# A diffusion trunk layer: its first norm taken on token rows, and its first projection run with the k tile outermost

## What is computed

```python
mod = silu(cvec) @ w_ada + b_ada            # 6 vectors of D: sh1, sc1, g1, sh2, sc2, g2
h = x * rsqrt(mean(x * x, axis=-1) + EPS) * rms1_g * (1 + sc1) + sh1
u = h @ w_in                                # q, k, v, the pooling input, the conv input
```

## Time and profile before

| | |
|---|---|
| median of 3 runs | 3322.55 us (3313.8 to 3324.69) |
| profiled execution | 3326.58 us, span 3324.5 us |
| TensorE busy | 2942.1 us, 88% of the span |
| VectorE, ScalarE, GpSimd busy | 1978.3, 1460.9, 459.5 us |
| HBM traffic | 570.72 MB read, 28.31 MB written, 180 GB/s over the span |

### The profile page before, as it was taken

The page is one execution under the profiler, slowest core; times in us unless marked ns, Lnnn a source line. Parts: engine busy times, 40 slices in busy tenths (PEclk is TensorE's granted clock), DMA queues, the critical chain, the costliest instruction groups (busy, mean ns, idle before and its releaser), DMA issues.

```text
span 3324.5 us, 42592 instructions
## 1 busy us (share of the span) xinstructions
PE 2942.1 (88%) x16896; PEld 2267.9 (68%) x16896; DVE 1978.3 (60%) x1880; ACT 1460.9 (44%) x1588; POOL 459.5 (14%) x259
## 2 busy tenths in 40 slices
PE   5979887999985999999859798879999859999997
PEld 4978764887883666666549787648878836666664
DVE  3198874211135888888632988742111358888885
ACT  4135553211124677777442355432111246777774
POOL 0321110000001122122203211100000011222122
PEclk8989998999997999999979999889999979999998
DMA  6211124212125999999832111242222259999994
GB/s 239 69 55 45 45 72 169 77 64 64 64 89 187 335 367 380 370 367 379 305 124 58 53 45 45 96 146 77 64 64 64 89 202 335 375 374 369 373 373 165
DMA packets 238382, 601.12 MB, mean 181 GB/s; under 512 B 13536, under 2 KB 116096, under 8 KB 237472
## 3 DMA queue, kind: packets, MB, share of 16 engines
q1 hardware_dynamic: 224896, 549.09, 45.4%
q0 software_dynamic: 10272, 34.26, 4.0%
q10 hardware_dynamic: 3072, 15.73, 1.2%
HBM read 570.72 MB, written 28.31 MB: 180 GB/s over the span
## 4 chain that ended last, share of the span: by engine, by line
PE 78%; DVE 11%; DMA 5%; ACT 2%; issue 2%; SPq 1%; POOL 0%; DVEq 0%; ACTq 0%; POOLq 0%; PEldq 0%
PE ps L1254 19%; PE ps L1255 19%; PE ps L1256 19%; PE ps L1292 8%; DVE zc L941 4%; DMA raw<-in_w_ada 2%; PE ps L1417 2%; PE ps L1393 1%; DMA xg<-h_dram,next_token 1%; PE ps L1567 1%; PE ps L1406 1%; DMA raw<-in_w_in 1%; PE ps L1337 1%; DVE w_lo L850 1%; DVE stats L971 1%
## 5 line engine op out<-in xcount | busy, mean ns | idle before, releaser
L1254 PE MATMUL ps<-h_hi,w_hi 128*128 128x320 f32 x1408 | 448.3, 318 | 81.1 <-DVE h_lo L899 48.0
L1169 DVE TENSOR_TENSOR m_lo<-m_raw_b,m_hi 128x2048 fp32r<-128x2048 f32 x192 | 439.4, 2289 | 73.4 <-ACT m_hi L794 71.6
L1169 DVE TENSOR_TENSOR m_lo<-m_raw_a,m_hi 128x2048 fp32r<-128x2048 f32 x192 | 438.8, 2288 | 69.7 <-ACT m_hi L794 67.7
L794 ACT CAST m_hi<-m_raw_b 128x2048 fp32r<-128x2048 f32 x192 | 367.1, 1912 | 179.0 <-PE ps L1256 179.0
L1255 PE MATMUL ps<-h_lo,w_hi 128*128 128x320 f32 x1408 | 441.2, 313 | 0.0
L1256 PE MATMUL ps<-h_hi,w_lo 128*128 128x320 f32 x1408 | 440.8, 313 | 0.0
L794 ACT CAST m_hi<-m_raw_a 128x2048 fp32r<-128x2048 f32 x192 | 366.4, 1911 | 164.6 <-PE ps L1256 161.5
L1254 PE MATMUL ps<-m_hi,xs_hi 128*80 128x512 f32 x1024 | 409.1, 400 | 3.3 <-DVE xs_lo L1184 3.3
L1255 PE MATMUL ps<-m_lo,xs_hi 128*80 128x512 f32 x1024 | 406.4, 397 | 0.0
L1256 PE MATMUL ps<-m_hi,xs_lo 128*80 128x512 f32 x1024 | 404.4, 395 | 0.0
L500 ACT CAST w_hi<-raw 128x2048 fp32r<-128x2048 f32 x68 | 129.2, 1902 | 552.4 <-DMA raw<-in_w_gate 335.7
(11 more groups left out here) (257 smaller groups left out, 4744.7 us busy)
## 6 DMA issues: line engine op xcount, KB each, us to landing
m_raw_a<-in_w SPq DMA_DIRECT2D x192, 1024.0 KB, 7.4
m_raw_b<-in_w SPq DMA_DIRECT2D x192, 1024.0 KB, 7.4
raw<-in_w_in SPq DMA_DIRECT2D x72, 512.0 KB, 4.7
raw<-in_w_ada SPq DMA_DIRECT2D x64, 512.0 KB, 4.7
raw<-in_w_gate SPq DMA_DIRECT2D x48, 512.0 KB, 6.2
m_raw_a<-in_w_ada SPq DMA_DIRECT2D x8, 1024.0 KB, 9.6
m_raw_b<-in_w_ada SPq DMA_DIRECT2D x8, 1024.0 KB, 15.6
raw<-in_w_proj_a SPq DMA_DIRECT2D x16, 512.0 KB, 4.1
```

The costliest lines, as they stand in the source:

```text
L794: nc.scalar.copy(m_hi[:, n % RING], m_raw(slot)).then_inc(s["m_high"], 1)
L1169: nc.vector.tensor_tensor(m_lo[:, r], m_raw(slot), m_hi[:, r].bitcast(F32), ALU.subtract).then_inc(s["msplit"], 1)
L1254: pe.matmul(out, wh, xh, start=first, stop=False, skip_group_check=True)
```

## The change

The row scale 1/rms of the first norm is taken from `xtok`, by token rows, where it is one number per partition: ScalarE squares a token tile with a running sum (`accum_out`), VectorE and ScalarE finish the five numbers per tile on [128, 1] columns, and VectorE scales `xtok` in place (`row_scales`), after TensorE has turned the unscaled tile for `x`. TensorE then turns the scaled `xtok` again, k tile by k tile, into two PSUM halves (`turn_h`), ScalarE applies scale and shift while it reads PSUM and writes a new tile `hm`, casts it at once (`high_of`), VectorE subtracts (`low_of`). The first unit (`pool_first`) runs with the k tile outermost and takes each tile as its low part is done; tile k+2 is turned between the matmuls of tile k and tile k+1. The other units run as before; the loop of three passes becomes one written-out pass and a loop of two.

Around it: x is loaded in five DMAs, one per token tile with a semaphore each, by SP in both layers; in layer 1 SP waits for the last scatter itself. The layer's constants `sm` and the first unit's weight chunk go ahead of the eight `w_ada` chunks in SP's queue, and POOL loads neither x nor constants. In layer 1 both weight splits stand ahead of the row statistics; in layer 0 the first stands behind them and the second between h tiles 2 and 3. PSUM banks of the first modulation part move from 6 and 7 to 0 and 1. The second norm of a layer is left as it was.

The diff, cut to its core:

```diff
             sp.dma_start(c_in[:], cvecs).then_inc(s["const_in"], 16)
             sp.dma_start(fold[:], fold_in).then_inc(s["const_in"], 16)
-            sp.dma_start(xtok[:, 0:4, :], x_sample[0].rearrange("(t p) d -> p t d", p=P)).then_inc(s["x_in"], 16)
-            sp.dma_start(xtok[:, 4, :], x_prompt[0]).then_inc(s["x_in"], 16)
+
+            def load_x(lat, ctx):
+
+                for t in range(TT):
+                    src = lat[t * P:(t + 1) * P] if t < 4 else ctx
+                    sp.dma_start(xtok[:, t, :], src).then_inc(s[f"x_in{t}"], 16)
+
+            load_x(x_sample[0], x_prompt[0])
+            sp.dma_start(sm[:], small[0]).then_inc(s["small_in"], 16)
             sp.sem_inc(s["raw_free0"], 1)
             sp.sem_inc(s["raw_free1"], 1)
...
+            def first_wide(l):
+
+                wide(0, in_v[l, POOL0 // CW])
+
+            first_wide(0)
+            for i in range(RAWS):
+                sp.dma_start(m_raw(i), ada_chunk(0, 0, i)).then_inc(s[f"mfull{i}"], 16)
             for l in range(DEPTH):
                 for n, c0 in enumerate((POOL0, CONVB0, CONVA0)):
                     for u in range(2):
-                        wide(u, in_v[l, c0 // CW + u])
+                        if n + u:
+                            wide(u, in_v[l, c0 // CW + u])
+                    if l and n == 0:
+
+                        sp.wait_ge(s["scattered"], 32 * EXPERTS * l)
+                        seen.settle()
+                        load_x(mid_lat, mid_ctx)
...
                 if l + 1 < DEPTH:
+                    sp.wait_ge(s["small_free"], l + 1)
+                    sp.dma_start(sm[:], small[l + 1]).then_inc(s["small_in"], 16)
+                    first_wide(l + 1)
                     for i in range(RAWS):
                         sp.wait_ge(s["msplit"], seen("msplit"))
...
-                pool.wait_ge(s["small_free"], seen("small_free"))
-                seen.settle()
-                pool.dma_start(sm[:], small[l]).then_inc(s["small_in"], 16)
...
-                    pool.dma_start(xtok[:, 0:4, :], mid_lat.rearrange("(t p) d -> p t d", p=P)).then_inc(s["mid_in"], 16)
-                    pool.dma_start(xtok[:, 4, :], mid_ctx).then_inc(s["mid_in"], 16)
...
-                bank = (6, 6, 7)[n]
+                bank = (0, 6, 7)[n]
...
-            def h_high(k):
-
-                act.wait_ge(s["hnorm"], seen("hnorm"))
-                nc.scalar.copy(h_hi[:, k], mm_[:, k]).then_inc(s["row_c"], 1)
+            def x_out(t):
+
+                act.wait_ge(s["tr_in"], TT * l + t + 1)
+                b = 2 * (t % 2)
+                nc.scalar.copy(x[:, :, t * P:(t + 1) * P], flat[:, b * 512:b * 512 + D].rearrange("p (k n) -> p k n", n=P)).then_inc(s["tr_out"], 1)
+
+            def x_stats():
+
+                for t in range(TT):
+                    act.wait_ge(s[f"x_in{t}"], 16 * (l + 1))
+                    nc.scalar.activation(xsq[:, t], xtok[:, t], ACT.Square, accum_out=st[:, 8 + t:9 + t]).then_inc(s["x_sq"], 1)
+                    if t:
+                        x_out(t - 1)
+                    act.wait_ge(s["x_var"], TT * l + t + 1)
+                    nc.scalar.activation(st[:, 13 + t:14 + t], st[:, 8 + t:9 + t], ACT.Sqrt).then_inc(s["x_root"], 1)
+                x_out(TT - 1)
+                act.wait_ge(s["tr_out"], TT * (l + 1))
+                act.dma_start(x_dram, x[:].rearrange("p k n -> p (k n)")).then_inc(s["x_saved"], 16)
+
+            def high_of(k):
+
+                act.wait_ge(s["h_full"], KT * l + k + 1)
+                nc.scalar.copy(h_hi[:, k], hm[:, k]).then_inc(s["h_high"], 1)
+
+            def first_h(between):
+
+                act.wait_ge(s["mods_ready"], seen("mods_ready"))
+                for k in range(KT):
+                    act.wait_ge(s["xn_ps"], KT * l + k + 1)
+                    b = 4 + 2 * (k % 2)
+                    for c, (a, e) in ((1, (0, LAT)), (0, (LAT, TOK))):
+                        ins = nc.scalar.activation(hm[:, k, a:e], flat[:, b * 512 + a:b * 512 + e], ACT.Identity,
+                                                   scale=coef[:, k, c:c + 1], bias=mods[:, k, c:c + 1])
+                    ins.then_inc(s["h_full"], 1)
+                    high_of(k)
+                    if k == 2:
+                        between()
...
-                if shift == 0:
-                    if l == 0:
-                        ada_out(0)
-                    split_high(0, 0)
-                    split_high(1, 1)
...
                 if l:
                     ada_out(0)
-                for k in range(KT):
-                    act.wait_ge(s["tr_in"], seen("tr_in"))
-                    b = 2 * (k % 2)
-                    nc.scalar.copy(x[:, k], flat[:, b * 512:b * 512 + TOK]).then_inc(s["tr_out"], 1)
-                act.wait_ge(s["tr_out"], seen("tr_out", KT))
-                act.dma_start(x_dram, x[:].rearrange("p k n -> p (k n)")).then_inc(s["x_saved"], 16)
-                norm(0, l)
+                    split_high(0, 0)
+                    split_high(1, 1)
+                    x_stats()
+                    first_h(lambda: None)
+                else:
+                    x_stats()
+                    split_high(0, 0)
+                    ada_out(0)
+                    first_h(lambda: split_high(1, 1))
...
                 dve.wait_ge(s["small_in"], seen("small_in", 16))
+
+                def row_scales():
+
+                    for t in range(TT):
+                        dve.wait_ge(s["x_sq"], TT * l + t + 1)
+                        nc.vector.tensor_scalar(st[:, 8 + t:9 + t], st[:, 8 + t:9 + t], 1.0 / D, EPS, ALU.mult, ALU.add).then_inc(s["x_var"], 1)
+                        dve.wait_ge(s["x_root"], TT * l + t + 1)
+                        link(nc.vector.reciprocal(st[:, 18 + t:19 + t], st[:, 13 + t:14 + t]))
+                        dve.wait_ge(s["tr_in"], TT * l + t + 1)
+                        nc.vector.tensor_scalar(xtok[:, t], xtok[:, t], st[:, 18 + t:19 + t], None, ALU.mult).then_inc(s["x_norm"], 1)
+
+                def low_of(k):
+
+                    dve.wait_ge(s["h_high"], KT * l + k + 1)
+                    return nc.vector.tensor_tensor(h_lo[:, k], hm[:, k], h_hi[:, k].bitcast(F32), ALU.subtract).then_inc(s["h_low"], 1)
+
+                if l:
+                    add_mods(0)
+                    coefficients(8, "rms1")
+                    split_low(0, 0)
+                    split_low(1, 1)
+                    row_scales()
+                else:
+                    row_scales()
+                    split_low(0, 0)
+                    add_mods(0)
+                    coefficients(8, "rms1")
                 lv = small_at("lam_vec").rearrange("p (a b n) -> p a b n", a=2, b=2)
                 link(nc.vector.tensor_tensor(row2[:, 0:128].rearrange("p (a n) -> p a n", a=2), lv[:, :, 0, :], lv[:, :, 1, :], ALU.mult))
                 nc.vector.tensor_reduce(st[:, 0:2], row2[:, 0:128].rearrange("p (a n) -> p a n", a=2), AX.X, ALU.add).then_inc(s["lam_a"], 1)
-                if l:
-                    add_mods(0)
-                norm()
-                if l == 0:
-                    add_mods(0)
-                coefficients(8, "rms1")
-                split_low(0, 0)
-                split_low(1, 1)
                 for k in range(KT):
-                    dve.wait_ge(s["row_c"], seen("row_c"))
-                    ins = nc.vector.tensor_tensor(h_lo[:, k], mm_[:, k], h_hi[:, k].bitcast(F32), ALU.subtract)
-                ins.then_inc(s["hready"], 1)
+                    low_of(k)
+                    if l == 0 and k == 2:
+                        split_low(1, 1)
...
                 ins.then_inc(s["av"], 1)
 
             def turn_x():
-                pe.wait_ge(s[("x_in", "mid_in")[l]], 32)
+
+                for t in range(TT):
+                    pe.wait_ge(s[f"x_in{t}"], 16 * (l + 1))
+                    if TT * l + t >= 2:
+                        pe.wait_ge(s["tr_out"], TT * l + t - 1)
+                    b = 2 * (t % 2)
+                    for k in range(KT):
+                        ins = pe.transpose(flat[:, b * 512 + k * P:b * 512 + (k + 1) * P], xtok[:, t, k * P:(k + 1) * P], ident[:])
+                    ins.then_inc(s["tr_in"], 1)
+
+            def turn_h(k):
+
+                pe.wait_ge(s["x_norm"], TT * (l + 1))
+                if KT * l + k >= 2:
+                    pe.wait_ge(s["h_full"], KT * l + k - 1)
+                b = 4 + 2 * (k % 2)
+                for t in range(TT):
+                    ins = pe.transpose(flat[:, b * 512 + t * P:b * 512 + (t + 1) * P], xtok[:, t, k * P:(k + 1) * P], ident[:])
+                ins.then_inc(s["xn_ps"], 1)
+
...
+            def pool_first():
+
                 for k in range(KT):
-                    if k >= 2:
-                        pe.wait_ge(s["tr_out"], seen("tr_out"))
-                    b = 2 * (k % 2)
-                    for t in range(TT):
```

(37 more changed lines are left out.)

35 lines of the change are left out of this document (14 added, 21 removed).

## The result

The changed kernel took 3273.61 us (median of 4 runs, 3269.58 to 3282.0) beside 3323.62 (4 runs) of the kernel before: ratio 0.9859, 95% interval 0.983 to 0.9888. The profiled execution took 3282.0 (span 3280.2), 44.3 us of span less than the one before.

The account below looks back on a forecast made before the run. The prediction took the chain as bound by TensorE (78%), with time to win where it leaves matmuls. Gains of 5.7 us (layer 0) and 29.6 (layer 1), 35.3 in all, off the median 3322.55 gave 3287, range 3274 to 3306.

Parts of the forecast that it names:

- The first unit: First projection unit of each layer: a 5.5 us loop per two tiles, 24.3 us in layer 0, 22.6 in layer 1.
- the row statistics: Layer 1, from x's landing: 2.4 us per token tile on ScalarE, 12.3 us for five, last root at 1676.3.
- The ring's last chunk: Layer 0 modulation: the last of eight chunks lands at 43.5, putting `mods_ready` at 46.4.
- the second rival: Both first units stay at the lower clock, 32.4 us each; gain 17.4 us, time 3305; chance 0.11.
- The third rival: Layer 0's constants land with the modulation chunks instead of ahead; loss 14.1 us there, time 3307; chance 0.05.
- E: End of each layer's first projection unit: 73.5 in layer 0 (gain 5.7 us), 1704.3 in layer 1 (gain 29.6 us).
- What E gains is kept unless something behind it has a date of its own. I find none: Behind E: units run back to back and weight slots move with E, so the 35.3 us gain is kept.
- the fourth rival: ScalarE keeps up and the first-unit loop hides, units of 19 us; gain 48.5 us, time 3274; chance 0.08.
- the fifth rival: No change: something behind E with a date of its own absorbs the gain; time 3322; chance 0.04.

Follow-up runs that it names:

- before_placed: Kernel before the change, with 154 already fulfilled waits at the head of TensorE's list, where it waits for x; 3308.78 us, ratio 0.9953.
- k_outer_only: Kernel before the change, with only the first unit's k tile made outermost, following each h tile's subtraction; norm and loads unchanged; 3298.24 us, ratio 0.9928.
- again: The changed kernel run once more with no edit; 3268.31 us, ratio 0.9838.
- turn_first: Changed kernel, with the turn of h tile k+2 issued ahead of the matmuls of tile k in the first unit; 3264.21 us, ratio 0.9825.
- rows_only: Changed kernel, with all h tiles turned first and the first unit run output by output, leaving only the token-row norm; 3281.9 us, ratio 0.9879.
- x_two_loads: Changed kernel, with x loaded by two transfers (four row tiles and one) instead of five; 3274.11 us, ratio 0.9848.
- after_pad: Changed kernel, with 128 already fulfilled waits in TensorE's layer 0 list to shift its later code; 3275.52 us, ratio 0.9849.
- after_placed: Changed kernel, with fulfilled waits only where TensorE idles, so both merge loops start at 0.60 of a 256-instruction step; 3266.84 us, ratio 0.9832.
- best_placed: The kernel of best, with its fulfilled waits moved to places where TensorE idles anyway; 3257.55 us, ratio 0.9799.
- before_pad: Kernel before the change, with 246 already fulfilled waits in TensorE's list where it waits for the layer 0 ring; 3321.17 us, ratio 0.9996.
- best: Changed kernel, with layer 0's h tiles turned and copied to SBUF early, layer 1's turns ahead of matmuls, and 348 and 164 fulfilled waits; 3275.26 us.
- after: The changed kernel as first measured, against the kernel before the change; 3273.61 us, ratio 0.9859.

## Why the prediction was right, and what it left out

**Layer 0, start.** The ring's last chunk was used at 43.56 (43.5 forecast). Its matmuls took 1.98 us and the fold 1.05, where the forecast had 1.07 and 0.65 from the earlier trace rows: TensorE was at a mean clock of 0.62 there, and this the forecast missed. Before, the matmuls with ones kept TensorE busy for 10.54 us, from 21.66, right ahead of the ring; the change removed them, and the ring alone, waiting between chunks, did not hold the clock. Where those matmuls are kept and the ring waits for its last chunk (before, before_placed, k_outer_only) the last 16 matmuls took 1.07 us; where they are gone and it waits (the changed kernel, again, turn_first, rows_only, x_two_loads, after_pad, after_placed, best_placed) they took 1.70 to 1.98. No run puts them back into the changed kernel. The rows:
```profile
36.00:50.00 14.00, 7.47 (x68) 2.96 (x64) 1.45 (x6) 2.78 (x5) 0.00 (x0) 0.62 0.88 314
50.40:53.40 3.00, 2.96 (x11) 2.99 (x12) 0.82 (x1) 0.80 (x2) 0.00 (x0) 0.52 0.00 0
53.40:74.00 20.60, 16.80 (x117) 15.71 (x115) 7.62 (x9) 14.26 (x21) 1.10 (x6) 1.00 0.16 52
```
So `mods_ready` came at 47.53, not 46.4, and TensorE at 50.45, not 49.2. From the first Identity to the first matmul it took 2.89 (2.8 forecast).

**The first unit.** 23.74 us in layer 0 (24.3 forecast) and 22.85 in layer 1 (22.6); two tiles take 5.41 (5.5), and turn_first and best_placed show that this loop and the second split set the length. The clock was low for the first 3 us and 1.00 after them, with TensorE busy 16.80 of 20.60 us. So the second rival is out. The loop that the Trainium skill, TensorE: Matmul & The Clock Gate, "HAM oscillation — how this bites in real kernels", describes loses its clock at each k tile, but there the wait for the next tile is longer than the tile's matmuls. That is not this loop's case, so the prediction read the section too widely, and nothing here speaks against it. The third rival is out too: VectorE had the constants at 12.88 (17.4 forecast).

**Layer 1.** The forecast started the row statistics at the landing of x and had both weight splits hidden behind it. The chain goes another way: over the `w_ada` ring, which TensorE runs only behind the last expert product, the casts and the two splits.
```profile
1648.86 7.09 PE ps L1363 x128
...
1658.17 2.30 DVE w_lo L890
1660.61 2.30 DVE w_lo L890
```
VectorE was free at 1662.9, and ScalarE's first root waited 0.95 us for it; with x in one large transfer the statistics waited for x instead (x_two_loads). The price was small, and other terms were too large. The first square began 10.95 us behind Y, not 12.0. The statistics took 2.04 us a tile, not 2.4: root, square and copy run one behind the other on ScalarE with nothing between (1663.24, 1663.44, 1664.48 in the chain above, the next root at 1665.28), which is 4 x 0.36 = 1.4 us less. From the last root to TensorE's first matmul it took 4.8, not 5.4. In all TensorE started 27.5 us behind Y instead of 29.7, the unit took 0.25 longer, and layer 1's gain was 31.6 instead of 29.6.

**Behind E.** "What E gains is kept unless something behind it has a date of its own. I find none" is the step that failed, and in both directions. Layer 0 loses there. In its attention stage TensorE takes the later `w_ada` chunks, and the chain goes through one load of them after another, 4.7 to 7.1 us each in the changed kernel. When the first of these chunks is used the changed kernel is 6.4 us ahead; at the fold behind the last it is 0.7 ahead (TensorE's timeline, before and after):
```profile
488.95 1.47 PE L1302 MATMUL ps<-raw,cs_in_zeros 128*32 128x256 f32 x16
...
548.62 0.62 PE L1330 MATMUL ps<-fold,ada_rows_scale_gate 128*128 128x16 f32 x4 [0.63 <-ACT ada_rows_scale_gate L509]
```
```profile
482.52 1.46 PE L1363 MATMUL ps<-raw,cs_in_zeros 128*32 128x256 f32 x16
...
547.89 0.76 PE L1391 MATMUL ps<-fold,ada_rows_scale_gate 128*128 128x16 f32 x4 [0.63 <-ACT ada_rows_scale_gate L527]
```
That stretch took 59.7 us before and 65.4 after, but 62.2 in the second execution of the changed kernel (again). In the four traces that reach it at 487 or later it took 59.7 to 61.9, in the nine that reach it earlier 62.2 to 68.4. So a part of layer 0's gain is lost there; how large a part one pair of traces can't tell, and why, no run shows. Just ahead of layer 0's merge stage the profiled pair had minus 0.4 left of 5.04, again 1.8 of 4.26 against the same trace, the placed pair 2.3 of 4.8, and best_placed 6.5 of 6.9 against after_placed. In layer 1 the profiled pair kept its gain, but the stretch from E to the conv matmuls that end the merge loop's first pass took 658.6 to 672.0 us in the thirteen traces, so there too one pair shows little.

In the other direction, 14.1 us (3.0 and 11.1 in the two merge stages; 3.0 and 10.4 of them from the start of the second pass on) came from a loop that the change doesn't touch, because its code moved: shown by the kernel that repeats it (again), by waits that bring the idle time into the changed kernel (after_pad) and by waits that take it out of the kernel before (before_placed) and out of layer 0 (best, after_placed).

**What was luck.** The forecast was right on its own terms at the first units (36.6 for 35.3). The whole time was not: 3273.61 is the fourth rival's 3274 almost exactly, but not by its way, as the units took 23.7 and 22.9 us and not 19; the merge loop's place made up most of the difference. And TensorE's first matmul of layer 1 at 1676.40, where the prediction named 1676, is two errors that cancel: layer 0 had handed on 3.1 us at Y and not 5.7, and the start came 2.2 us earlier behind Y. One slip in the chances: the fifth rival and what is left of the third make 0.06, not 0.05.

**What stays open.** Which places are good: 0.60 of a step was good in the changed kernel's layer 1 and in both layers of best, after_placed and best_placed, and bad in before_pad; 0.42 and 0.48 were good in before_placed, as guessed. These places are my counts of the built program, and no trace shows them. And of the 42 us between the placed kernels 35.2 are at the first units; of the other 7 I can say only that one and the same kernel's median moved by 5 us from one group of runs to the next (after and again).

## What to carry to other kernels

Where one tile goes through TensorE, ScalarE and VectorE and back, write the loop down as a sum and issue the next tile's turn ahead of this tile's matmuls: that took 5.1 and 3.5 us off the two first units. A statistic moved to another layout pays where its input comes last (layer 1, 24.9 us alone) and costs where something else does (layer 0, minus 2.4 alone). And before a difference of under 1% is put down to an edit, follow the gain along both traces to the end: a stage that the edit doesn't touch may have changed because code ahead of it grew.

## What the runs showed of the hardware

At the start of a loop's second pass TensorE stood idle for 0.9 us with no packet of the instruction queue, or for 4.9 to 8.8 us with 2 to 4 of them, depending on where the loop's code lies. With the low clock behind it a bad place cost 5 to 11 us a loop; placing both loops well made the kernel before 15.9 us faster. A fulfilled wait on TensorE took 52 to 53 ns where many stand in a row (246 in 12.75 us, 348 in 18.44); the 128 of after_pad left a gap of only 4.65 us. And matmuls that look like a cost may hold the clock for the work behind them: without the sums of squares the ring's last 16 matmuls took 1.70 to 1.98 us in place of 1.07, in every run where the ring waits for that chunk.
